# Passages between layers: TensorE takes the first tile's share of the next layer while the second tile is normed, and the low halves of the weights lie over their slabs

## The reference

```python
x = x + rmsnorm(mixer(rmsnorm(x, g0), ...), g1)          # first block
x = x + rmsnorm(swiglu(rmsnorm(x, g2), ...), g3)
for i in range(2):                                       # second block
    mod = (silu(c) @ ada_w[i] + ada_b[i])[:, None, :]
    sh_a, sc_a, g_a, sh_f, sc_f, g_f = split(mod, 6)
    h = rms_norm(x, norm_g[i, 0]) * (1.0 + sc_a) + sh_a
    y = moba_attention(h, ...) if i == 0 else diff_attention(h, ...)
    x = x + g_a * rms_norm(y, norm_g[i, 1])
    h = rms_norm(x, norm_g[i, 2]) * (1.0 + sc_f) + sh_f
    x = x + g_f * rms_norm(swiglu_2(h, ...), norm_g[i, 3])
```

## Time and profile before

| | |
|---|---|
| median of 3 runs | 1032.81 us (1031.98 to 1033.02) |
| the profiled execution | 1032.01 us, its span 1030.4 us |
| PE busy | 993.9 us, 96% |
| DVE busy | 686.2 us, 67% |
| ACT busy | 493.6 us, 48% |
| DMA, mean over the span | 219 GB/s |
| chain that ended last | PE 92%, DVE 4%, ACT 2% |

### The profile page before, as it was taken

The page is one execution under the profiler, slowest core; times in us unless marked ns, Lnnn a source line. Parts: engine busy times, 40 slices in busy tenths (PEclk is TensorE's granted clock), DMA queues, the critical chain, the costliest instruction groups (busy, mean ns, idle before and its releaser), DMA issues.

```text
span 1030.4 us, 16100 instructions
## 1 busy us (share of the span) xinstructions
PE 993.9 (96%) x6814; PEld 913.7 (89%) x6814; DVE 686.2 (67%) x980; ACT 493.6 (48%) x689; POOL 28.9 (3%) x49
## 2 busy tenths in 40 slices
PE   5999999989999998999989999998999989999998
PEld 4988999879998997999889999997997779999997
DVE  5766666787757676787676556567998684545443
ACT  6644533564343345555564343436666574343341
POOL 1000000000000001000000000001000010000000
PEclk9999999999999999999989999999999989999999
DMA  9853577549896875696537666663866337465501
GB/s 374 346 183 114 183 251 257 197 149 350 308 288 225 304 276 187 222 354 225 200 121 275 220 240 215 238 244 124 330 247 221 126 106 280 163 205 167 202 1 41
DMA packets 32871, 225.65 MB, mean 219 GB/s; under 512 B 3949, under 2 KB 4229, under 8 KB 6304
## 3 DMA queue, kind: packets, MB, share of 16 engines
q1 hardware_dynamic: 30960, 219.53, 59.4%
q0 software_dynamic: 1552, 4.88, 1.4%
q10 hardware_dynamic: 288, 0.22, 0.1%
HBM read 223.54 MB, written 1.08 MB: 218 GB/s over the span
## 4 chain that ended last, share of the span: by engine, by line
PE 92%; DVE 4%; ACT 2%; issue 1%; DMA 1%; POOL 0%; SPq 0%; DVEq 0%
PE psum L565 20%; PE psum L566 19%; PE psum L567 19%; PE psum L591 9%; PE psum L592 9%; PE psum L593 9%; PE psum L745 2%; PE psum L306 1%; DVE low L495 1%; ACT work_v L337 1%; PE psum L811 1%; DMA raw<-in_v 1%; ACT lam_pr L960 1%; DVE x_res L415 1%; DVE raw L504 0%
## 5 line engine op out<-in xcount | busy, mean ns | idle before, releaser
L495 DVE TENSOR_TENSOR low<-raw,high 128x2048 fp32r<-128x2048 f32 (+1 forms) x160 | 363.4, 2276 | 180.5 <-ACT high L487 180.5
L565 PE MATMUL psum<-h_hi,high 128*128 128x256 f32 x1600 | 458.5, 287 | 0.0
L566 PE MATMUL psum<-h_lo,high 128*128 128x256 f32 x1600 | 454.7, 284 | 0.0
L567 PE MATMUL psum<-h_hi,low 128*128 128x256 f32 x1600 | 454.4, 284 | 0.0
L487 ACT ACTIVATE high<-raw 128x2048 fp32r<-128x2048 f32 (+1 forms) x160 | 302.4, 1900 | 74.9 <-PE psum L593 64.0
L565 PEld LDWEIGHTS psum<-h_hi,high 128*128 128x128 f32 x1600 | 309.0, 193 | 6.3 <-issue 2.8
L566 PEld LDWEIGHTS psum<-h_lo,high 128*128 128x128 f32 x1600 | 309.1, 193 | 1.4 <-issue 0.2
L567 PEld LDWEIGHTS psum<-h_hi,low 128*128 128x128 f32 x1600 | 308.9, 193 | 0.0
L591 PE MATMUL psum<-high,y_hi 128*128 128x512 f32 x328 | 128.8, 393 | 0.0
L592 PE MATMUL psum<-low,y_hi 128*128 128x512 f32 x328 | 128.0, 390 | 0.0
L593 PE MATMUL psum<-high,y_lo 128*128 128x512 f32 x328 | 127.7, 389 | 0.0
(11 more groups left out here) (155 smaller groups left out, 740.4 us busy)
## 6 DMA issues: line engine op xcount, KB each, us to landing
raw<-in_gate_up SPq DMA_DIRECT2D x66, 1024.0 KB, 5.1
raw<-in_ada SPq DMA_DIRECT2D x48, 1024.0 KB, 5.5
raw<-in_down SPq DMA_DIRECT2D x33, 1024.0 KB, 5.4
raw<-in_mix SPq DMA_DIRECT2D x14, 1024.0 KB, 5.8
raw<-in_moba_qk SPq DMA_DIRECT2D x8, 1024.0 KB, 6.0
raw<-in_diff_qk SPq DMA_DIRECT2D x8, 1024.0 KB, 6.3
raw<-in_qk SPq DMA_DIRECT2D x4, 1024.0 KB, 15.2
raw<-in_branch SPq DMA_DIRECT2D x4, 1024.0 KB, 4.9
```

What stands on the lines that cost most here:

```text
L495: nc.vector.tensor_tensor(low[n % N_LO][:, s], raw[i % N_RAW][:, s], high[n % N_HI][:, s].bitcast(F32), ALU.subtract).then_inc(*rest.up(key))
L565: nc.tensor.matmul(to, a, hi(k), start=first, stop=False)
L566: nc.tensor.matmul(to, a, lo(k), start=False, stop=False)
L567: m = nc.tensor.matmul(to, r, hi(k), start=False, stop=last and j > j0)
```

## The change

1. Buffers. `raw` has eight places and `high` six; `low` is now written over the slab it comes from, so there are eight of it and none apart. A load waits until PE has used the slab eight places back.
2. The three last downs of each FFN stand together at its end, behind the last up.
3. Tile 0's turn (`pe_turn(stage, 0)`) stands inside tile 1's matmuls of the closing layer, with 12 matmuls behind it. `pe_wide` takes its last three slabs in one pass, tile 0 of all three first.
4. The first gate and up of an FFN are done tile by tile in a third form, `pe_rows` (a tile of h stands still, 256 columns of weights move); the turn of tile 1 stands between the two tiles. The hidden rows are then turned by four transposes (`pe_turn_rows`). In both attentions the values slabs 0 and 1 come first, with the turn of tile 1 between the tiles; for diff they stood behind q and k before.
5. ACT's and DVE's programs at the passages follow this order; the lowered leads are gone.
6. The end of the diff attention is written in another order: the first two applied pairs follow the turn of head 4, ahead of values 2.

```diff
-N_RAW, N_HI, N_LO = 6, 4, 4
+N_RAW, N_HI = 8, 6
...
-            if g:
+            if 0 < g < FG - 2:
                 order.append((down, base * FG + g - 1))
-        return order + [(down, base * FG + FG - 1)]
+        return order + [(down, base * FG + g) for g in range(FG - 3, FG)]
...
-                yield from sp.wait_ge(*((rest, b) if before == "main" else (summed, b)))
+                yield from sp.wait_ge(*((slab, b) if before == "main" else (summed, b)))
...
-            if n >= N_LO:
-                yield from dve.wait_ge(slab, n - N_LO)
-            nc.vector.tensor_tensor(low[n % N_LO][:, s], raw[i % N_RAW][:, s], high[n % N_HI][:, s].bitcast(F32),
+            nc.vector.tensor_tensor(low[i % N_RAW][:, s], raw[i % N_RAW][:, s], high[n % N_HI][:, s].bitcast(F32),
...
+            yield from pe_moving(name, [wide_part(WIDE[0])], data, ready, KC // 2, KC, freed_by_norm(stage), name, first)
+            parts = [wide_part(index) for index in WIDE[1:]]
+            turn = {(1, 0, 1): lambda: pe_turn(stage, 0)}
...
+            for a in range(2):
+                n = NUM[gate_up, base * 2 * FG + a * FG]
...
+                for k in range(KC):
+                    yield from pe.wait_ge(h_lo_made, (before, t, k))
+                    hi, lo = h_hi[:, k, tile_of(t)], h_lo[:, k, tile_of(t)]
+                    nc.tensor.matmul(to, hi, wh[:, k, :], start=a == 0 and k == 0, stop=False)
...
         def pe_ffn(f, meanwhile={}):
...
+            yield from pe_rows(f, 0)
+            yield from pe_turn(before, 1)
+            yield from pe_rows(f, 1)
+            for g in range(1, FG):
...
+            yield from pe_down(f, FG - 3, FG - 2, FG - 1, between=turn)
...
-            for i in range(2):
-                yield from dve_next(down, base * FG + FG - 2 + i, AHEAD - i)
+            yield from dve_next(down, base * FG + FG - 1)
...
-                for i, index in enumerate(WIDE[2:]):
-                    yield from dve_next(name, index, AHEAD - i - hold)
+                for index in WIDE[2:]:
+                    yield from dve_next(name, index)
...
                     yield from dve_attend(tag, 6)
-                    yield from dve_next(v, 1)
+                    yield from dve_apply_pairs((0, 4), (2, 6))
+                    yield from dve_next(v, 2)
+                    yield from dve_scale_pairs(0, 2)
                     yield from dve_attend(tag, 7)
...
                     yield from pe_attend(tag, 6)
-                    yield from values(1)
-                    yield from pe_attend(tag, 7)
-                    yield from values(2, {(0, 0): lambda: pe_apply_pairs((0, 4), (2, 6))})
+                    yield from pe_apply_pairs((0, 4), (2, 6))
+                    yield from values(2, {(0, 0, 1): lambda: pe_attend(tag, 7)})
```

More of the change, by code:

```diff
@@ L376, in act_post_norm, with square_y, square_x @@
                 yield from act.wait_ge(signal, key)
[L377 to L384, removed]
+            def square_y(t, c):
+                yield from act.wait_ge(slab, ("sum", tag, t, c))
+                act_square(psum[4 + 2 * t + c][:, :], ("y", stage, t, c), t, c, 4)
+            def square_x(t):
                 for c in range(2):
@@ L404, in dve_post_norm, with make_x @@
             yield from dve.wait_ge(*gain_ready(POST[stage][1]))
[L405 to L408 removed]
+            def make_x(t):
                 yield from dve_join(("y", stage, t), t, 4)
@@ new lines, in act_row, with dve_row @@
+        def act_row(f, t):
+            yield from act.wait_ge(slab, ("row", f, t, 1))
+            nc.scalar.activation(row_tmp(t, 0), psum[bank_of["rows", f, t]][:, 0:S], ACT.Silu).then_inc(
+                *evacuated.up(("silu row", f, t)))
+        def dve_row(f, t):
+            yield from dve.wait_ge(evacuated, ("silu row", f, t))
+            nc.vector.tensor_tensor(row_tmp(t, 1), psum[bank_of["rows", f, t]][:, S:2 * S], row_tmp(t, 0), ALU.mult).then_inc(
+                *produced.up(("row", f, t)))
@@ new lines, in pe_turn_rows, with act_turn_rows @@
+        def pe_turn_rows(f):
+            o = yield from bank(("turned rows", f), (hi_made, ("hidden", f, 0)), (lo_made, ("hidden", f, 0)))
+            for t in range(NT):
+                yield from pe.wait_ge(produced, ("row", f, t))
+                for k in range(2):
+                    m = nc.tensor.transpose(o[:, k * S + t * P:k * S + (t + 1) * P], row_tmp(t, 1)[:, k * P:(k + 1) * P], ident)
+            m.then_inc(*turned.up(("hidden", f)))
+        def act_turn_rows(f):
+            yield from act.wait_ge(turned, ("hidden", f))
+            yield from act.wait_ge(slab, Y_USED[f])
+            nc.scalar.activation(y_hi[:, 0:2, :], pair(bank_of["turned rows", f]), ACT.Copy).then_inc(*hi_made.up(("hidden", f, 0)))
@@ L647, in pe_ffn @@
                     yield from meanwhile[g]()
-            yield from pe_down(f, FG - 2, FG - 1)
+            turn = {(1, 0, 1): lambda: pe_turn(behind, 0)} if behind != 5 else {}
+            yield from pe_down(f, FG - 3, FG - 2, FG - 1, between=turn)
         def act_ffn(f):
             gate_up, down, base, _, _ = FFN[f]
-            for g in range(FG):
+            yield from act_row(f, 0)
+            yield from act_next(gate_up, base * 2 * FG, AHEAD)
+            yield from act_row(f, 1)
+            for g in range(1, FG):
                 gate, up = (gate_up, base * 2 * FG + g), (gate_up, base * 2 * FG + FG + g)
```

235 lines of the change are left out of this document (123 added, 112 removed).

## The result

The changed kernel takes 1037.33 us (median of 4 runs, 1036.52 to 1039.21) against 1032.39 us of the kernel before beside it: ratio 1.0055, 95% interval [1.0043, 1.0067]. It is slower by 4.9 us between the medians, and by 4.4 to 6.9 us by the interval; 1038.3 us had been forecast. Its profiled span is 1035.8 us against 1030.4.

A forecast was written before the change was run, and what follows sets the result against it. PE, busy 96%, was taken as the bound, leaving its waits and clock losses. Terms 1.8 - 2.0 - 4.8 + 0.5 + 0 + 10.0 = +5.5 on 1032.01 gave 1037.5, with the median's 0.8 1038.3 us; range 1018 to 1045.

The forecast's parts named there:

- Passages 2 and 3: Last up to moba's first q, -2.0 us; last pass of moba_o to first down, -4.8; short idles, clock holds.
- The end of the diff attention: Scores of head 5 to diff_o: PE idles 7.2 us for a DVE chain; +10.0 us, bounds +5 and +12.
- The 1.0 later on: End of the diff attention: 1.0 us because the second turn's pairs reach DVE behind a sum.
- Passage 1: Out1 to the first down: four splits ahead of the norm, transposes at 209.1, 8.2 us against 6.4, +1.8.
- one piece of 5.2 us: Passage 1: PE wants tile 0's transposes at 203.85, has them at 209.1, so idles 5.2 us.
- The clock at passage 1: Behind passage 1's idle: the clock stands at half, costing 2.0 us.
- Passage 4: Last up to the scores of head 0, modulation slab on DVE: idle 4.2 us, clock falls, 7.2 against 6.7, +0.5.
- Passage 5: Last pass of diff_o to first down: transposes wait 0.8 us, tile 0's rows some 3.2, clock's 2.8 about unchanged; 0.
- Buffers: Low over raw, later loads, six high places: taken at 0; upper bounds +5.5 for splits, +4 for loads.
- a sign that it was wrong: Whole kernel: the forecast is wrong if, among other signs, loads end waits of ACT.
- Cover that holds everywhere: Rival: passages lose some 2.4 us each, 12.2 for 32.4, diff tail nothing; 1012 or 1010 us, chance 0.13.
- The fall of the clock at passages 2 and 3: Rival: short idles with transposes behind them cost the clock, 2 us each, 1042.3, up to 1046 with late loads; chance 0.15.

The follow-up runs named there:

- e1: Kernel before with only the buffers' part of the change (eight raw, six high, low written over its slab, later loads): 1032.31 us, ratio 1.0009.
- e5: Changed kernel with the weighing of heads 5 and 6 ahead of the first applied pairs, and on DVE those pairs' scaling ahead of the next split: 1035.58 us.
- e9: Changed kernel with the diff attention in the order of the kernel before, values 0 and 1 behind q and k: 1039.59 us, ratio 1.0067.
- the repeat: Second profile of the changed kernel, run again with no edit on the same chip as the others: 1037.28 us, ratio 1.0054.
- e3: Changed kernel with DVE's and ACT's lead lowered by one slab ahead of each norm: 1031.74 us, ratio 1.0001 to the kernel before.
- e6: Changed kernel with e3's lower lead, e4's passage 5 order, and the left-out slab rounded and split inside the norm: 1038.56 us, ratio 1.0072.
- e7: Changed kernel with the edits of e6 and e5 together: 1034.83 us, ratio 1.0037 to the kernel before.
- e2: Changed kernel with exponentials and weighing of heads 5 and 6 ahead of the first applied pairs on ACT and DVE: 1035.84 us, ratio 1.0040.
- e10: Changed kernel with the edits of e9, e3 and e4, and the next slab's rounding and split ahead of the first rows' silu and product: 1030.19 us.
- e4: Changed kernel with passage 5 in the other passages' order, tile 0's h parts, scale and shift moved earlier: 1032.87 us, ratio 1.0014.

## Why the prediction was right, point by point

- **Passages 2 and 3** (-2.0 and -4.8 forecast, -2.2 and -4.3 measured): idle 1.5 and 0.9 us where 1.8 and 1.3 had been worked out, and the clock held. But the 4.8 us put down for passage 2 before contain a fall of the clock that e1 doesn't have behind the same idle; against e1 the passage gives 0.6 us. That -2.0 met -2.2 is partly luck of the profile. Passage 3 gave 0.5 us less than forecast; behind tile 1's transposes its rows wait 0.6 us for ACT's scale and shift, which I hadn't counted.
- **The end of the diff attention** (+10.0; +9.3 and +10.2): the idle was put at 7.2 us and is 6.78, that of head 4's turn at 0.8 and is 1.17, the clock at 0.50 behind it. The 1.0 later on has its match in 1.08 us for y_lo at 821.71. What the prediction had not settled, why the cover is gone, e5 and e9 narrow down: the order of pairs and weighing alone gives 3 to 4 us back, the old order together with the two values slabs 7 to 8. The two figures overlap and don't add.
- **Passage 1** (+1.8): the transposes were put at 209.1 and stand at 208.12, with the timeline 0.93 us earlier since the start of the kernel (out1 begins at 183.75, before at 184.68). Taken from there the place is met; the shift itself is not the change's, since e1 has 0.8 of it. But one step failed. The idle was put in one piece of 5.2 us; 1.5 of it come earlier, since the single pass over three slabs wants the second of them 12 matmuls sooner:

```profile
196.46 0.50 PE L602 MATMUL psum<-high,h_hi 128*128 128x512 f32 x1 [1.52 <-DVE low L506]
```

- **The clock at passage 1** was the other: 2.0 us of loss were taken as certain. The first profile has none, the repeat has them, and +1.8 lies between +0.4 and +3.1 by luck (between -0.7 and +2.0 against e1).
- **Passage 4** (+0.5, measured -0.1): idle 3.78 in place of 4.2.
- **Passage 5** (0; +1.9 and -0.2): the transposes' wait of 0.8 us is not there at all, the rows' 3.2 us are 2.79 and 0.91 to 1.27. The clock's part, put at what it was before, is there in the first profile and missing in the repeat.
- **Buffers** (0, bounds to +5.5 and +4): e1 has them at nothing that could be told from noise, within 2 us. Loads do come later: ACT's rounding waits 52.9 us for them in the changed kernel, 18.4 of it for gate and up slabs, and 1.2 us before. The prediction had named this as a sign that it was wrong, and on this point it was: the slack of about four slabs' time was not there at these places. It cost little, since ACT runs ahead of PE; the one wait of PE that can come of it has 0.9 us, in the diff attention (the fifth line of the table, 0.2 us in the repeat).
- **The rivals.** Cover that holds everywhere would have given 1010: each norm had one split more ahead of it, and e3 shows what that split costs. The fall of the clock at passages 2 and 3 was not seen in the changed kernel: the eight transposes behind idles of 1.5 and 0.9 us took 1.06 us, as at full clock. The rule of the Trainium skill ("TensorE: Matmul & The Clock Gate", section "Part 4: PE-mode transpose") that transposes don't count as work that keeps the clock up therefore had no price here. Nor do speak for it: the clock was at 0.50 from the first of those transposes on, so that the idle ahead of them explains it by itself. The rival was nearer than it looks, though: in e6 and e7, with idles of 2.0 us at these two passages, the clock fell at both.

The mechanism was right: wins and losses were worked out at their own places, and the idles stand there with the lengths given. That the sum hit within 1 us is luck: the clock alone moves passages 1, 2 and 5 by 1.1 to 2.7 us each from one profile to another.

## What to carry to other kernels

Cover put under a stall is worth only what isn't eaten by work let in ahead of the chain that ends the stall: here a lead lower by one slab ahead of each norm turned 5.6 us of loss into none, while the end of the diff attention stayed as it was. Work moved to cover one stall is taken from somewhere: count what it covered there, on the engine that waits. And after each such edit read which wait is next; in e2, e5, e6 and e10 the wait removed had a new one in its place within 20 us.

## What the runs showed of the hardware

The granted clock behind the same idle isn't the same from one execution to the next. At passage 1 the changed kernel has PE idle for 3.2 us. In its first profile (windows of 2 us; the column ahead of the last two is the granted clock):

```profile
206.00:208.00 2.00, 0.00 (x0) 0.00 (x0) 0.67 (x3) 1.13 (x4) 0.55 (x1) 1.00 0.80 279
208.00:210.00 2.00, 1.88 (x13) 1.73 (x14) 1.49 (x4) 1.21 (x5) 0.00 (x0) 1.00 0.96 401
```

and in the repeat, with the same program:

```profile
206.00:208.00 2.00, 0.00 (x0) 0.00 (x0) 0.52 (x2) 1.28 (x5) 0.55 (x1) 0.78 0.95 291
208.00:210.00 2.00, 1.72 (x9) 1.75 (x9) 1.12 (x3) 0.60 (x3) 0.00 (x0) 0.50 0.97 410
```

The stretch takes 53.31 us in the one and 55.99 in the other: 2.7 us for the clock's fall from its full level (2.4 GHz) to half of it (1.2 GHz). At the same idle of 3.2 us e2, e5 and e9 have the fall, e4 hasn't. After the idles of 3.8 us at passage 4, of 5.4 us in e9 and e10 and of 6.8 us at the turn of head 5 the clock was at 0.50 in every profile; at passage 4 of the repeat it fell only 0.9 us after the idle had ended, with the transposes done in 1.09 us. After the idles of 1.5 us and less at passages 2 and 3 it fell in none. Between them lie idles that had either: of 2.58 us in the kernel before a fall and of 2.59 us in e1 none, of 1.92 us at passage 1 a fall in e7 and none in e6, of 2.19 us at the last pass of diff_o a fall in e9 and none in e10. In the changed kernel itself passage 5 (2.8 us idle, then 0.9 to 1.3) differs between its two profiles by 2.2 us in the same way. For an idle like these an estimate can only give both values.
